# Inverse roots of norms on GpSimd: one power operation in place of a ScalarE root refined on VectorE

## The reference, cut to what matters

```python
def rms_norm(x, g):
    y = xf * lax.rsqrt(jnp.mean(xf * xf, axis=-1, keepdims=True) + EPS)
    return (y * g).astype(x.dtype)

def group_layer_norm(x, n_groups, g, b=None):      # mean over the width of a group
    y = (xc * lax.rsqrt(var + EPS)).reshape(shp) * g

for l in range(DEPTH):                             # first block, DEPTH = 2
    h = rms_norm(x, g_pre_mix[l]) * (1 + sc_mix) + sh_mix
    y = mixer(h, ...)                              # holds both group norms:
    #   h_m = group_layer_norm(h_m, H, g_mh)                      4 heads of 256
    #   a = silu(group_layer_norm(a, N_CONV_GROUPS, g_cn, b_cn))  8 groups of 128
    x = x + gt_mix * rms_norm(y, g_post_mix[l])
    h = rms_norm(x, g_pre_mlp[l]) * (1 + sc_mlp) + sh_mlp
    f = square(relu(h @ w_ff1[l])) @ w_ff2[l]
    x = x + gt_mlp * rms_norm(f, g_post_mlp[l])
...
return rms_norm(x, final_norm_w)                   # end of the second block
```

## Time and profile before

| | |
|---|---|
| median of 3 runs | 2281.36 us (2279.96 to 2281.94) |
| span of the profiled execution, first to last instruction | 2274.4 us |
| median minus that span (start and end of an execution) | 7.0 us |
| TensorE busy | 2222.0 us, 98% |
| VectorE / ScalarE / GpSimd busy | 1280.8 / 992.0 / 1131.6 us |
| mean granted TensorE clock | 0.994 of full |

### The profile page before, as it was taken

One profiled execution on the slowest core, in us unless ns is written; L12 is line 12 of the kernel. 1 busy time (PEld: TensorE's weight loads), 2 busy tenths in 40 slices (PEclk: granted clock), 3 DMA queues, 4 the chain that ended last, 5 costly groups with the idle time before them and its releaser, 6 DMA issues.

```text
span 2274.4 us, 28727 instructions
## 1 busy us (share of the span) xinstructions
PE 2222.0 (98%) x10450; PEld 1749.5 (77%) x10450; DVE 1280.8 (56%) x2061; ACT 992.0 (44%) x1630; POOL 1131.6 (50%) x596
## 2 busy tenths in 40 slices
PE   8999999999999999999999999999999999999998
PEld 5886667788888878766778888887767688888886
DVE  4999847863546699984365122157776653221222
ACT  4368543333232335875344223244666653331323
POOL 2698833554444639876374344463422244444442
PEclk9999999999999999999999999999999999999999
DMA  8432205354646323221122323232222122333332
GB/s 319 138 98 71 65 29 172 120 185 157 231 166 217 96 77 94 75 84 38 56 84 86 99 93 101 87 108 72 82 57 65 47 92 94 103 92 97 97 99 86
DMA packets 206662, 240.39 MB, mean 106 GB/s; under 512 B 9762, under 2 KB 172378, under 8 KB 206554
## 3 DMA queue, kind: packets, MB, share of 16 engines
q1 hardware_dynamic: 205990, 238.76, 32.9%
q10 hardware_dynamic: 564, 0.21, 0.0%
HBM read 236.84 MB, written 2.10 MB: 105 GB/s over the span
## 4 chain that ended last, share of the span: by engine, by line
PE 52%; DVE 3%; POOL 2%; issue 2%; ACT 1%; DMA 0%; DVEq 0%; POOLq 0%; ACTq 0%; SPq 0%
PE product L2508 16%; PE product L2510 15%; PE product L2509 15%; DVE side L1888 1%; PE side L3076 1%; POOL ring_low L950 1%; PE product L3111 1%; POOL slot_f L981 1%; PE side L3096 1%; POOL slot_f L1003 1%; PE product L2881 1%; PE side L2865 0%; PE side L3023 0%; DVE slot_f L1888 0%; ACT sqt L1436 0%
## 5 line engine op out<-in xcount | busy, mean ns | idle before, releaser
L950 POOL TENSOR_TENSOR ring_low<-ring_f,ring_high 128x1024 fp32r<-128x1024 f32 (+1 forms) x349 | 845.6, 2427 | 1029.2 <-ACT ring_high L1076 1028.8
L2508 PE MATMUL product<-slot_r,ring_high 128*128 128x512 f32 (+1 forms) x2536 | 1007.1, 397 | 13.5 <-ACT slot_f L1282 4.0
L2510 PE MATMUL product<-slot_r,ring_high 128*128 128x512 f32 (+1 forms) x2536 | 989.3, 390 | 0.0
L2509 PE MATMUL product<-slot_r,ring_low 128*128 128x512 f32 (+1 forms) x2536 | 988.3, 390 | 0.0
L1076 ACT ACTIVATE ring_high<-ring_f 128x1024 fp32r<-128x1024 f32 (+1 forms) x349 | 367.8, 1056 | 697.9 <-DMA ring_f<-in_w_ff 326.0
L2508 PEld LDWEIGHTS product<-slot_r,ring_high 128*128 128x128 f32 (+1 forms) x2536 | 475.9, 188 | 146.4 <-issue 35.5
L2510 PEld LDWEIGHTS product<-slot_r,ring_high 128*128 128x128 f32 (+1 forms) x2536 | 475.9, 188 | 101.5
L2509 PEld LDWEIGHTS product<-slot_r,ring_low 128*128 128x128 f32 (+1 forms) x2536 | 476.4, 188 | 97.0 <-issue 1.4
L1845 DVE SCALAR_TENSOR_TENSOR va<-product,sqt 128x512 f32<-128x512 f32 x96 | 66.3, 692 | 332.9 <-ACT sqt L1154 331.6
L1888 DVE SCALAR_TENSOR_TENSOR side<-slot_f,cols,side 128x512 f32<-128x512 f32 x322 | 214.8, 747 | 0.0
L1865 DVE TENSOR_TENSOR slot_f<-product,slot_f 128x512 f32<-128x512 f32 x64 | 44.2, 691 | 161.6 <-PE product L2510 161.6
(11 more groups left out here) (325 smaller groups left out, 2164.8 us busy)
## 6 DMA issues: line engine op xcount, KB each, us to landing
ring_f<-in_w_ff SPq DMA_DIRECT2D x128, 512.0 KB, 3.8
slot_f<-in_w_ada SPq DMA_DIRECT2D x48, 1024.0 KB, 7.4
ring_f<-in_w_in SPq DMA_DIRECT2D x96, 512.0 KB, 3.9
ring_f<-in_w_out SPq DMA_DIRECT2D x40, 512.0 KB, 3.4
ring_f<-in_w_up SPq DMA_DIRECT2D x32, 512.0 KB, 3.7
ring_f<-in_w_down SPq DMA_DIRECT2D x32, 512.0 KB, 3.6
slot_f<-in_x SPq DMA_DIRECT2D x4, 512.0 KB, 5.0
ring_f<-in_w_v SPq DMA_DIRECT2D x4, 512.0 KB, 3.5
```

The source lines that it names most:

```text
L950: pool.tensor_tensor(whole(ring_low[:, s, :, :], n), whole(ring_f[:, s, :, :], n), whole(ring_high[:, s, :, :], n).bitcast(F32), ALU.subtr ...
L2508: pe.matmul(out_ap, high, rhs_high, start=start, stop=False)
L2509: pe.matmul(out_ap, low, rhs_high, start=False, stop=False)
L2510: return pe.matmul(out_ap, high, rhs_low, start=False, stop=stop)
```

## The change

Every inverse root that used ScalarE's `Sqrt`, except the very first one of the program, becomes one GpSimd `tensor_tensor` with `ALU.pow`: the variance plus EPS, now written by VectorE into SBUF (`root`), to the power of a column of -0.5 (`neg_half`). VectorE makes a variance where ScalarE did a root, and loses its four refining instructions; ScalarE loses the roots and their dummy roots, and five table loads in all. The means of x's squares are kept (`x_means`) in place of the sums. TensorE loses the single dummy product between the two spreads of a boundary. GpSimd gets eight 128x4 operations at boundaries (two each), four of 128x128 in the layers and one 128x4 at the end, each behind a wait and ahead of what follows in its list.

```diff
+            def inverse_root(y, v, signal):
+
+                pool.tensor_tensor(y, v, neg_half.to_broadcast([P, v.shape[1]]), ALU.pow).then_inc(signal.sem, 1)
+
+            def boundary(place, b):
+
+                wait(pool, place, y_var, b + 1)
+                inverse_root(inv_cols[:, 0:BLK], root[:, 0:BLK], y_rstd)
+                wait(pool, place, x_var, b + 1)
+                inverse_root(inv_cols[:, BLK:2 * BLK], root[:, BLK:2 * BLK], x_rstd)
 
...
+                wait(pool, place, cvar_ready, 1)
+                inverse_root(inv_cols[:], root[:], crn_small)
                 for hd in range(HEADS):
                     add_probs(hd)
...
                                        ALU.add).then_inc(pair_sums.sem, 1)
+                wait(pool, place, hvar_ready, 1)
+                inverse_root(inv_cols[:], root[:], hrn_small)
                 for i in range(I_OUT + AHEAD + HEADS, I_FF):
                     low_part(place, LAYER, i)
...
+                    if i == I_FF + 2:
+                        boundary(place, 0)
                     low_part(place, LAYER, i)
...
+            pool.wait_ge(final_ready.sem, BLK + 1)
+            inverse_root(final_inv, root[:, 0:BLK], r_small)
...
-                square_root_next()
-                wait(act, place, y_summed, b + 1)
-                deviation(place, y_totals, D, y_root)
                 weights(NT - 1)
-                wait(act, place, x_summed, b + 1)
-                deviation(place, x_sums, D, x_root, BLK)
 
...
-                wait(dve, place, y_root, b + 1)
-                settled(dve)
-                steps.did(dve.tensor_scalar(v, by_kind[:, 0, :], 1.0 / D, EPS, ALU.mult, ALU.add))
-                inverse_root(v, q, root[:, 0:BLK], r_out, y_rstd)
+                wait(dve, place, y_summed, b + 1)
+                dve.tensor_scalar(v_out, by_kind[:, 0, :], 1.0 / D, EPS, ALU.mult, ALU.add).then_inc(y_var.sem, 1)
                 wait(dve, place, y_rstd, b + 1)
-                steps.did(dve.tensor_tensor(w, by_kind[:, 1, :], r_out, ALU.mult))
+                steps.did(dve.scalar_tensor_tensor(u, by_kind[:, 1, :], 1.0 / D, r_out, ALU.mult, ALU.mult))
                 steps.wait()
                 wait(dve, place, cross_summed, b + 1)
-                steps.did(dve.scalar_tensor_tensor(u, PB[1][:, 0:BLK], 2.0, w, ALU.mult, ALU.add))
+                steps.did(dve.scalar_tensor_tensor(u, PB[1][:, 0:BLK], 2.0 / D, u, ALU.mult, ALU.add))
                 steps.wait()
                 steps.did(dve.tensor_tensor(u, u, r_out, ALU.mult))
                 steps.wait()
-                steps.did(dve.tensor_tensor(u, u, x_sums, ALU.add))
+                steps.did(dve.tensor_tensor(u, u, x_means, ALU.add))
                 steps.wait()
-                dve.tensor_scalar(x_sums, u, 0.0, None, ALU.max).then_inc(x_summed.sem, 1)
-                wait(dve, place, x_summed, b + 1)
-                steps.did(dve.tensor_scalar(v, x_sums, 1.0 / D, EPS, ALU.mult, ALU.add))
+                dve.tensor_scalar(v_x, u, 0.0, EPS, ALU.max, ALU.add).then_inc(x_var.sem, 1)
+                steps.did(dve.tensor_scalar(x_means, u, 0.0, None, ALU.max))
                 wait(dve, place, y_spread, b + 1)
                 scaled(0)
-                wait(dve, place, x_root, b + 1)
-                settled(dve)
-                inverse_root(v, q, root[:, BLK:2 * BLK], r_x, x_rstd)
+                steps.wait()
                 moved(0)
                 wait(dve, place, x_spread, b + 1)
                 for t in range(NT):
@@ -1927,6 +1929,7 @@
             wait(dve, Place(), root_ready, 1)
             settled(dve)
...
-                wait(dve, place, croot_ready, 1)
-                settled(dve)
-                refine(PM[2], P, P, crn_small)
+                wait(dve, place, cvar, 2)
+                dve.tensor_scalar(root[:], PM[2][:, 0:P], 1.0 / P, EPS, ALU.mult, ALU.add).then_inc(cvar_ready.sem, 1)
...
-                v, q = (PM[3][:, k * P:(k + 1) * P] for k in (2, 3))
-                dve.scalar_tensor_tensor(v, PM[3][:, 0:P], 1.0 / (2 * P), met, ALU.mult, ALU.add).then_inc(hvar_ready.sem, 1)
-                wait(dve, place, hroot_ready, 1)
-                settled(dve)
                 wait(dve, place, crn_ready, NT)
-                inverse_root(v, q, root[:], inv_cols[:], hrn_small)
+                dve.scalar_tensor_tensor(root[:], PM[3][:, 0:P], 1.0 / (2 * P), met, ALU.mult, ALU.add).then_inc(hvar_ready.sem, 1)
...
-            v, q, first_half = (PM[3][:, k * P:k * P + BLK] for k in (2, 3, 1))
+            first_half = PM[3][:, P:P + BLK]
             steps.did(dve.tensor_scalar(first_half, square_cols(1), 1.0 / D, EPS, ALU.mult, ALU.add))
             for n in range(BLK, 2 * BLK):
                 add_rows(inner, n, lambda o, s: dve.wait_ge(rows_done.sem, s + 1))
             dve.wait_ge(root_ready.sem, 1 + 2 * BLK)
             steps.wait()
-            dve.scalar_tensor_tensor(v, square_cols(2), 1.0 / D, first_half, ALU.mult, ALU.add).then_inc(final_ready.sem, 1)
-            dve.wait_ge(final_ready.sem, BLK + 1)
-            dve.wait_ge(root_ready.sem, 2 + 2 * BLK)
-            inverse_root(v, q, root[:, 0:BLK], final_inv, r_small)
+            dve.scalar_tensor_tensor(root[:, 0:BLK], square_cols(2), 1.0 / D, first_half, ALU.mult, ALU.add).then_inc(final_ready.sem, 1)
             wait(dve, place, r_small, 2)
             for s in range(BLK):
                 dve.scalar_tensor_tensor(out_rows[:, s, T:D], XT[:, s, T:D], final_inv[:, s:s + 1], final_gain[:, T:D],
@@ -2632,7 +2627,6 @@
                 ins.then_inc(cross_summed.sem, 1)
                 wait(pe, place, y_rstd, b + 1)
...
                 spread(PM[1], inv_cols[:, 0:BLK]).then_inc(y_spread.sem, 1)
-                keep_busy(PB[0], 1)
                 wait(pe, place, x_rstd, b + 1)
                 spread(PM[2], inv_cols[:, BLK:2 * BLK]).then_inc(x_spread.sem, 1)
```

More of the change, by code:

```diff
@@ L387, in program @@
         idle = small[:, 4:5]
+        neg_half = small[:, 5:6]
         a_cols = small[:, 8:24]
@@ L390, in program @@
         x_sums = small[:, 56:60]
+        x_means = small[:, 24:28]
         neg_ident = small[0:HEADS, 60:64]
@@ L511, in program @@
         cross_summed = Signal(sem("residual_products_summed"), 2)
-        y_root = Signal(sem("output_root"), 2)
+        y_var = Signal(sem("output_variance"), 2)
         y_rstd = Signal(sem("output_rstd"), 2)
         y_spread = Signal(sem("output_rstd_spread"), 2)
-        x_summed = Signal(sem("residual_squares_summed"), 2)
-        x_root = Signal(sem("residual_root"), 2)
+        x_var = Signal(sem("residual_variance"), 2)
         x_rstd = Signal(sem("residual_rstd"), 2)
@@ L928, in _ @@
             pool.memset(one_col, 1.0).then_inc(pool_sem, 1)
+            pool.memset(neg_half, -0.5).then_inc(pool_sem, 1)
             pool.affine_select(out=ident[:], in_=ident[:], compare_op=ALU.not_equal, fill=1.0, base=0,
@@ L933, in _ @@
                                pattern=[[1, P]], channel_multiplier=-1).then_inc(pool_sem, 1)
-            pool.wait_ge(pool_sem, 11)
+            pool.wait_ge(pool_sem, 12)
             pool.sem_inc(consts.sem, 1)
@@ L1047, in _ @@
                 for i in range(AHEAD):
+                    if i == 2:
+                        boundary(place, 1)
                     low_part(following, plan, i)
@@ L1052, in _ @@
             pool.memset(mask_pair, 0.0).then_inc(pool_sem, 1)
-            pool.wait_ge(pool_sem, 12)
+            pool.wait_ge(pool_sem, 13)
             pool.affine_select(out=mask_own, in_=mask_own, compare_op=ALU.is_ge, fill=NEG, base=0,
@@ L1372, in _ @@
                     decay(0, j)
-                square_root_next()
-                wait(act, place, cvar, 2)
-                deviation(place, PM[2][:, 0:P], P, croot_ready)
                 for t in range(NT):
@@ L1401, in _ @@
                 ahead.of(place, I_OUT + 5)
-                wait(act, place, hvar_ready, 1)
-                act.activation(root[:], PM[3][:, 2 * P:3 * P], ACT.Sqrt).then_inc(hroot_ready.sem, 1)
                 conv_share(4)
@@ L1630, in last_rows @@
                     square_sums(1 + h, s, XT[:, s, h * T:(h + 1) * T], root_ready)
-                act.wait_ge(final_ready.sem, BLK + 1)
-                act.activation(root[:, 0:BLK], PM[3][:, 2 * P:2 * P + BLK], ACT.Sqrt).then_inc(root_ready.sem, 1)
                 wait(act, place, r_small, 2)
@@ L1769, in boundary @@
             def boundary(place, b, slot, n, gain, gain_next, move):
-                sums, beside = PM[3], PB[2]
-                v, q, u = (beside[:, k * BLK:(k + 1) * BLK] for k in range(3))
-                by_kind = sums[:, 0:2 * BLK].rearrange("p (s k) -> p k s", k=2)
-                r_out, r_x, w = inv_cols[:, 0:BLK], inv_cols[:, BLK:2 * BLK], root[:, 2 * BLK:3 * BLK]
+                by_kind = PM[3][:, 0:2 * BLK].rearrange("p (s k) -> p k s", k=2)
+                r_out = inv_cols[:, 0:BLK]
+                v_out, v_x, u = (root[:, k * BLK:(k + 1) * BLK] for k in range(3))
```

(1 more changed line is left out.)

5 lines of the change are left out of this document (1 added, 4 removed).

## The result

The changed kernel takes **2365.61 us** (median of 5, 2360.59 to 2370.7) against 2281.94 (2279.96 to 2282.41, 5 runs of the kernel before beside it): ratio 1.0371, 95% interval 1.0356 to 1.0385. It is 83.7 us slower. The forecast was 2275.8 us, with a range up to 2297, so the sign and the range are both missed.

What follows compares the result with a forecast made beforehand. The chain of roots and waits, not arithmetic, was what the change could shorten, with TensorE 98% busy. Gains 4.5 + 0.8 + 0.7 - 0.36 = 5.6 us gave 2275.8 us; own range 2273.3 to 2277.5, whole range up to 2297.

Steps and rivals of the forecast that it cites:

- The unknown: a power on GpSimd: All new inverse roots: no row shows a GpSimd power; estimated at 26 ns a column, two six-fold functions.
- far bound: GpSimd power: longest time allowed for, forty plain steps or 86 ns a column, giving T4 0.52 and T128 11.2 us.
- T128: Time of a 128x128 power on GpSimd, in group and head norms: estimated 3.5 us, floor 0.45.
- T4: Time of a 128x4 power on GpSimd, at boundaries and end: estimated 0.28 us, floor 0.19.
- Group norm: Roots before its spreads, slack 3.14 and 4.04 us in the two layers: cost 0.36 us, any excess paid one for one.
- Head norm: Root before its spreads: TensorE's whole 0.8 us wait gained, with T128 covered up to 5.0 us.
- The cost that the prediction drew from it for `x_means`: Each boundary: shared SBUF access could add up to T4 four times, 1.1 us, making the sum 4.5 instead of 5.6.
- Boundaries: Four boundaries: shorter root chain brings first normed tiles 6.5 us sooner together, of which 4.5 us reach the products.
- the cap by the dummies: Boundaries: dummies partly at half speed end after the product's inputs, capping gains at 0.9, 1.35, 1.25 and 1.05 us.
- rival 3: Boundaries: without the dummy between spreads the low clock lasts, about 2.9 us at a boundary less gains; 2280.5 us, chance 0.11.
- End: Last root, from variance to scaling: power starts the scaling sooner, gain 0.7 us, fully exposed.
- Rival 1: Slow power holds up both norms: balance nought at T128 5.6 us, 15 us slower (2296.5) at 9.3; chance 0.30.

Runs made afterwards that it cites:

- plain_op: The changed kernel with each power replaced by a GpSimd product of ones, same shapes and waits, output not the reference's: 2274.14 us, ratio 0.9974.
- narrow: The changed kernel with the 128x128 roots of group and head norm put back to ScalarE and VectorE, 128x4 powers kept: 2283.78 us, ratio 1.0008.
- group_power: The changed kernel with only the head norm's root put back to ScalarE and VectorE; the group norm keeps its power: 2330.33 us, ratio 1.0212.
- base_no_dummy: The kernel before without the dummy product between the two spreads of a boundary, nothing else changed: 2284.09 us, ratio 1.0009.
- widths: The kernel before with unused powers of 1 to 64 columns appended to GpSimd's list, to time a power alone; no whole-kernel time given.

## Why the prediction was wrong

**The step that failed** is "The unknown: a power on GpSimd". It took 26 ns a column because that was "built on the only iterative function in the trace", VectorE's reciprocal, and it set the far bound at 86. Measured are 158.5, six times the estimate. T128 is 20.75 us instead of 3.5, T4 1.01 instead of 0.28, and both lie beyond the far bounds of 11.2 and 0.52. The text itself said that the rows bear out neither count of steps. So the far bound bounded nothing, and the range, cut off at T128 = 9.3, had only that count behind it.

**Group norm.** "Everything over the slack is paid one for one" holds for the wait: with the measured T128 the working gives 2 x 20.75 - 3.14 - 4.04 = 34.3 us, and 34.4 were there. It does not hold for the time, of which the group norms cost 46.5. **Head norm.** Slack 5.0: 2 x (20.75 - 5.0) = 31.5, measured 31.5. Also right: the TENSOR_SCALAR beside GpSimd fell from 2.28 us to 0.23, as GpSimd stands idle then. In `plain_op` it is 0.23 too, and in `narrow` and `group_power`, where the low part of 2.39 us runs beside it again, 2.28. That agrees with the rule of the Trainium skill on the shared way into SBUF ("GPSIMD Engine Reference", section Key points). The cost that the prediction drew from it for `x_means` can't be judged here: at the second boundary of after that operation had ended (846.60 + 0.16) when the power began at 846.77, so the two did not run together.

**Boundaries.** The forecast was 4.5 us of gain; they cost 1.75. That `plain_op` gains 4.3 at T4 = 0.20 is in part luck. The working had 6.5 us at the first normed tiles and let the dummies take 2.0 of them. In `plain_op` the tiles gain 4.3, and the dummies take nothing. The third and fourth boundaries are short of the forecast at the tiles, 0.6 and 0.8 against 1.7 and 1.8, as the working went by the 1.03 us of before for their cross sums and they took 1.84. The step that the shorter chain reaches the first product is right; the cap by the dummies and the length of the cross sums are not. With T4 = 1.01 the condition "as long as T4 is under 0.5" fails: the second spread is waited for again, 0.70 us at VectorE. What remained, 0.31 to 0.45 us a boundary, is given back to the dummies at the low clock. That is rival 3, which added 2.9 us for three dummies at half speed and had a chance of 0.11; in after they run 2.2 and 2.4 us longer in two boundaries, where they take 4.95 and 5.29, and 1.5 and 1.4 in the others (4.23 and 4.24). `base_no_dummy` shows that the missing dummy does this by itself in the first two boundaries, and less in the others. It is a matter of 2 us and not of the result.

**End.** The forecast was 0.7 us, and the gain is nothing: handover, power and handover (0.08 + 1.01 + 0.05) are as long as the root and its refinement. With the plain operation the gain was 0.8, so T4 is again the whole difference.

**Rivals.** Rival 1, the slow power, is what happened. Its balance point (5.6 us) was not tested by any run; its price was worked out at 9.3, half of the true one. Its formula at the measured T128 and with the boundary and end gains at nought gives 65.8 us. It lacks a term: the clock behind each wait, 17 us over four of them, which the sum put at nothing. Rival 3 had looked for the clock at the missing dummy, where it costs some 2 us, and not at the long waits that rival 1 itself makes.

## What to carry to other kernels

Where the operation that a change rests on is in no row, a ratio borrowed from another engine bounds nothing. Ask first from which duration on the sign turns (by the working here 5.6 us for 128 columns, 44 ns a column), and leave the range open beyond it. A function with a cost by the column belongs where it has few columns and slack ahead of it; `plain_op` shows how to learn in one run whether it is the place or the function that costs. A long wait of TensorE can cost more than its length: count the work behind it at half the clock, here 17 us on 66. And a gain that agrees with its forecast confirms the working only if the terms agree too.

## What the runs showed of the hardware

- A power on GpSimd takes about 0.38 us and 158.5 ns a column (580 ns for 1 column, 10522 for 64, 20746 for 128), for 16 partitions as for 128 (`widths`, 16 columns: 2884 and 2896 ns). A product in the same place takes 0.20 us for 4 columns and 0.40 for 128, a fiftieth of the power at 128.
- After 17.7 us without work TensorE's granted clock was 0.50, and it stayed so for 16 us in which TensorE was busy throughout (302 to 318 in the group norm of layer 0); behind the 15.7 us of the head norm it stayed so for 6 us. With dummy products through the wait it was 1.00 behind it, and 5.4 us were saved up to the first output product.
- A 128x128 TENSOR_SCALAR of VectorE takes 2.28 us beside a GpSimd low part of 2.39 us (before, `narrow`, `group_power`) and 0.23 us with GpSimd idle (after, `plain_op`).
- At a boundary one dummy product of 1.9 us between two groups of tiny products changes the speed of the next three: 5.21, 4.63, 3.65 and 3.69 us without it, 2.75, 2.90, 2.75 and 2.85 with it.
